# Layer 1's first six input-projection chunks from split rows and split weights

## The reference

```python
def hybrid_layer(h, p_i, ...):
    n = rmsnorm(h, g_mix)
    z = n @ w_in                     # 1024 -> 2432 columns, for the three mixers
    ...
    zc = z[..., o4:]                 # mixer C: GLU, causal conv of 31 taps, LayerNorm, silu
    glu = zc[..., :D_C] * jax.nn.sigmoid(zc[..., D_C:])
    conv_c, new_c = causal_dwconv(glu, prev_c, w_conv_c)
    y_c = jax.nn.silu(layernorm(conv_c + b_conv_c, g_ln_c, b_ln_c))
    y = jnp.concatenate([rmsnorm(y_a, ...), rmsnorm(y_b, ...), rmsnorm(y_c, ...)], axis=-1)
    h = h + y @ w_o
    h = h + ffn(rmsnorm(h, g_ffn))   # layer 0: dense SwiGLU; layer 1: top-2 of 8 experts
    h = h + jax.nn.sigmoid(rmsnorm(h, g_ple) @ w_ple_gate) * (p_i @ w_ple_proj)
    return h, new_a, new_c, v
```

## Time and profile before

| | us |
|---|---|
| median of three runs | 1104.04 (1102.91 to 1104.72) |
| the profiled execution | 1101.71 |
| its span, first to last instruction | 1100.1 |
| TensorE busy | 1077.6 (98%) |
| VectorE busy | 878.3 (80%) |
| ScalarE busy | 660.3 (60%) |
| mean granted TensorE clock | 0.996 |

### The profile page before, as it was taken

The page is one execution under the profiler, slowest core; times in us unless marked ns, Lnnn a source line. Parts: engine busy times, 40 slices in busy tenths (PEclk is TensorE's granted clock), DMA queues, the critical chain, the costliest instruction groups (busy, mean ns, idle before and its releaser), DMA issues.

```text
span 1100.1 us, 16067 instructions
## 1 busy us (share of the span) xinstructions
PE 1077.6 (98%) x5837; PEld 928.4 (84%) x5837; DVE 878.3 (80%) x1241; ACT 660.3 (60%) x830; POOL 43.5 (4%) x58
## 2 busy tenths in 40 slices
PE   9998999999999999999999999999999999999996
PEld 8887899999999887778888888888888888878785
DVE  5897566566667788349989999899998999999775
ACT  2204344344454113248888888887888878888674
POOL 1000000000000000000000010000100000002000
PEclk9999999999999999999999999999999999999998
DMA  8432644645542442339999999999999999999910
GB/s 336 152 145 79 229 154 163 263 154 174 193 170 77 169 153 86 146 116 349 367 363 405 357 391 373 357 399 366 385 374 350 414 363 379 376 368 408 382 71 40
DMA packets 24196, 291.48 MB, mean 265 GB/s; under 512 B 3160, under 2 KB 3192, under 8 KB 7376
## 3 DMA queue, kind: packets, MB, share of 16 engines
q1 hardware_dynamic: 21040, 280.32, 66.6%
q0 software_dynamic: 3104, 10.46, 2.7%
HBM read 283.98 MB, written 6.79 MB: 264 GB/s over the span
## 4 chain that ended last, share of the span: by engine, by line
PE 94%; DVE 2%; ACT 2%; DMA 1%; issue 1%; POOL 0%; DVEq 0%; ACTq 0%; POOLq 0%
PE bank L711 18%; PE bank L665 16%; PE bank L669 15%; PE bank L668 15%; PE bank L738 7%; PE bank L735 7%; PE bank L739 7%; PE bank L751 3%; DMA ring<-wstream 1%; PE bank L609 1%; PE bank L593 1%; PE bank L574 1%; DVE wlo L1269 0%; PE bank L761 0%; ACT whi L881 0%
## 5 line engine op out<-in xcount | busy, mean ns | idle before, releaser
L1269 DVE TENSOR_TENSOR wlo<-ring,whi 128x1024 fp32r<-128x1024 f32 x384 | 460.2, 1220 | 49.2 <-ACT whi L881 41.9
L881 ACT ACTIVATE whi<-ring 128x1024 fp32r<-128x1024 f32 x384 | 405.0, 1060 | 83.7 <-PE bank L665 72.0
L665 PE MATMUL bank<-whi,gh_hi 128*128 128x512 f32 x512 | 204.5, 399 | 0.1
L669 PE MATMUL bank<-whi,gh_lo 128*128 128x512 f32 x512 | 199.8, 390 | 0.0
L668 PE MATMUL bank<-wlo,gh_hi 128*128 128x512 f32 x512 | 199.5, 390 | 0.0
L735 PE MATMUL bank<-gh_hi,whi 128*128 128x264 f32 x480 | 138.0, 288 | 0.0
L738 PE MATMUL bank<-gh_lo,whi 128*128 128x264 f32 x480 | 136.0, 283 | 0.0
L739 PE MATMUL bank<-gh_hi,wlo 128*128 128x264 f32 x480 | 135.9, 283 | 0.0
L665 PEld LDWEIGHTS bank<-whi,gh_hi 128*128 128x128 f32 x512 | 96.2, 188 | 21.8 <-DVE wlo L1269 3.4
L669 PEld LDWEIGHTS bank<-whi,gh_lo 128*128 128x128 f32 x512 | 96.1, 188 | 20.9
L668 PEld LDWEIGHTS bank<-wlo,gh_hi 128*128 128x128 f32 x512 | 96.3, 188 | 18.4
(11 more groups left out here) (261 smaller groups left out, 1327.0 us busy)
## 6 DMA issues: line engine op xcount, KB each, us to landing
ring<-wstream SPq DMA_DIRECT2D x130, 2048.0 KB, 8.3
y_rows<-work POOLq DMA_DIRECT2D x7, 512.0 KB, 8.1
ring<-wstream SPq DMA_DIRECT2D x1, 1536.0 KB, 10.1
h<-x_in SPq DMA_DIRECT2D x2, 528.0 KB, 4.1
y_out<-work SPq DMA_DIRECT2D x2, 528.0 KB, 3.0
par<-par_in SPq DMA_DIRECT2D x2, 494.5 KB, 7.6
c_sample<-xc POOLq DMA_DIRECT2D x2, 372.0 KB, 3.8
stc<-state_in SPq DMA_DIRECT2D x2, 360.0 KB, 9.5
```

What stands on the lines that cost most here:

```text
L665: mm = pe.matmul(out[:, :], xh, whi[:, pos, cols_], start=(k == 0), stop=False)
L669: mm = pe.matmul(out[:, :], xl, whi[:, pos, cols_], start=False, stop=(k == last))
L881: nc.scalar.activation(whi[:, q % SPLITS, :], quarter_at(q), ACT.Copy).then_inc(S["hi"], 1)
L1269: v.tensor_tensor(wlo[:, q % SPLITS, :], quarter_at(q), whi[:, q % SPLITS, :].bitcast(F32), ALU.subtract).then_inc(S["lo"], 1)
```

## The change

Layer 1's six `zc` chunks are made by `project` in place of `project_fp32`. Its rows come from `hid_hi` and `hid_lo`, which VectorE writes in layer 0's gate, after `gz[k]`, for all eight k. `gz` is still made, since the thirteen `zab` chunks stay in float32; their first one now has the wait for it. The six quarters of `zc` weights join the list of those to be split. By `dense_quarters`, the first three of them are split in the gate's chunks 5, 6 and 7, the others in the `zc` stage, after the evacuations of chunks 0, 1 and 2.

```diff
-FP32_Q = [N_ZC + N_ZAB + KP * KD // QBLOCKS + KD] * DEPTH
-FP32_FROM = [NEED[_b["zc"]] - 1 for _b in BASE]
+FP32_Q = [(N_ZC if _l == 0 else 0) + N_ZAB + KP * KD // QBLOCKS + KD for _l in range(DEPTH)]
+FP32_FROM = [NEED[_b["zc" if _l == 0 else "zab"]] - 1 for _l, _b in enumerate(BASE)]
...
-                project_fp32(B["zc"], N_ZC, gz, S["gh_mix"])
-                project_fp32(B["zab"], 2 * CB, gz)
+                if l == 0:
+                    project_fp32(B["zc"], N_ZC, gz, S["gh_mix"])
+                else:
+                    project(B["zc"], N_ZC, *mix, S["gh_zc"])
+                project_fp32(B["zab"], 2 * CB, gz, S["gh_mix"])
...
                 for c in range(CC):
                     evacuate(B["zc"] + 2 * c, pp[:, 2 * c, :])
+                    low_upto(dense_quarters(B["zc"] + 2 * c))
                     some_taps(6 if c else 0, c)
                     evacuate(B["zc"] + 2 * c + 1, pp[:, 2 * c + 1, :])
+                    low_upto(dense_quarters(B["zc"] + 2 * c + 1))
                     some_taps(2 if c else 0, c)
...
                         mix_gain(l + 1, k)
+                        gain(l + 1, "g_mix", k, L[l + 1]["gh_zc"], hid_hi, hid_lo)
                         low_upto(dense_quarters(B["ple"] + k))
```

More of the change, by code:

```diff
@@ L299, in build @@
             "mean", "centred", "squared", "variance", "root_v", "scaled", "ln_b", "vt", "vtok", "mixed",
-            "y_c", "y_a", "y_b", "ys_sq", "y_ms", "y_root", "y_normed", "sq_ffn",
+            "y_c", "y_a", "y_b", "ys_sq", "y_ms", "y_root", "y_normed", "gh_zc", "sq_ffn",
             "gh_ple", "sq_ple", "sig_ple", "tails", "w_sT")} for l in range(DEPTH)]
```

## The result

The change takes 1107.97 us, the median of six runs (1107.06 to 1108.38), against 1103.06 us for the kernel before in six runs: a ratio of 1.0042, with a 95% interval from 1.003 to 1.0054. On a second occasion it was 1108.93 against 1102.75, ratio 1.0057 (1.0045 to 1.007). So it is slower, by 5 to 6 us. The profiled execution took 1107.93 us; its span, first to last instruction, is 1106.3.

What follows compares the result with a forecast made beforehand. TensorE bounds the kernel, with VectorE the slower engine in layer 0's gate. VectorE's delay 7.9, matmuls -3.8 and clock 2.3 give +6.4 us: 1110.4 us against the median, 1108.1 against the profiled execution; range 1106.3 to 1112.7.

Steps and rivals of the forecast that it cites:

- What bounds it: TensorE holds 94% of the chain; in layer 0's gate VectorE is slower, and its lateness there delays TensorE equally.
- The pairs, 7 x 0.80: Layer 0's gate: two row-part instructions per chunk on VectorE, seven times ahead of the last evacuation, 5.6 us later.
- the splits, 2 x 1.13: Gate chunks 5, 6 and 7: weight splits on VectorE, two ahead of the last evacuation, delay it 2.26 us.
- The matmuls, -3.8: Layer 1's six zc chunks: three float32r matmuls per block in place of float32 take 3.8 us off TensorE.
- the estimate of 5.3 us: Layer 1's six zc chunks: saving if three passes replaced four; worked out but not used in the forecast.
- Layer 1's splits: Three splits on VectorE in layer 1: its waits for TensorE absorb the lateness, so nothing is added.
- the ring: Weight transfers and slots: no transfer added, later slots asked for no later relative to TensorE, so nothing.
- The clock, +2.3: Layers' border: TensorE's waits drop its clock to 1.2 GHz as layer 1 starts, costing 2.3 us, bounds 0 and 4.6.
- The first wait ahead of it: Layers' border: TensorE waits some 3.6 us for squares of line 1134, before some 1 us for the last.
- the rival that the clock stays: Layers' border: the clock stays at 2.4 GHz, so only +4.05 us, 1108.1 us; chance 0.25.
- Hidden pairs: Layer 0's gate: row parts hide in VectorE's waits; fully, -3.8 us, 1100.2 us, chance 0.05; partly, within 0.2%, chance 0.05.
- VectorE late in layer 1: Layer 1: VectorE cannot use its 6.6 us of waits, line 1535 is 8.4 us late, 1112.4 us; chance 0.05.

Runs made afterwards that it cites:

- the filled run: The change plus 13 and 3 small matmuls into an unused bank where TensorE waits for squares: 1106.87 us, ratio 1.0043; run again, 1106.90 us, 1.0035.
- without pairs: The change without the two row-part instructions per gate chunk and the wait for them, so layer 1 computes other values: 1100.77 us, ratio 0.9978 to before.
- the pairs alone: The kernel before plus the two row-part instructions per gate chunk, results unused, no new splits, float32 matmuls: 1109.97 us, ratio 1.0069 to before.
- the splits behind the gate: The change with only its first three weight splits moved behind the gate's last chunk: 1108.43 us, ratio 1.0037 to before.
- the best version: The change with high row parts on ScalarE, low parts in VectorE's sigmoid wait, first three splits behind the gate: 1099.63 us, ratio 0.9965 to before.

## Why the prediction was right

**What bounds it.** VectorE was the slower engine in the gate, with no slack to layer 1. Right: 5.57 us of pairs in the gate alone made mixer B's rows later by 5.57 us.

**The pairs, 7 x 0.80, and the splits, 2 x 1.13.** Predicted 5.6 + 2.26, measured 5.57 + 2.27 apart and 7.87 together. The estimate of 4.06 us a chunk was met (4.05), because the same pair in the same shapes stood elsewhere in the trace.

**The matmuls, -3.8.** With the clock held up, first split matmul to first float32 one took 378.01 - 360.29 = 17.7 us in the filled run, 3.6 us less than six chunks at 3.56. That is 0.2 short of 3.8, and the delay ahead of them, 4.02 + 3.6 = 7.7, is 0.2 short of 7.9; that the sum came out at +4.02 for +4.05 owes something to the two cancelling. (The prediction's 353.0 for layer 1's first matmul was the start of a piece of the chain; the matmul itself starts at 352.85.) The Trainium skill (FP8 and Floating Point Precision, TensorE Precision Notes) counts four passes for true float32; the estimate of 5.3 us worked out from that would have been too high beside the 3.6 measured.

**Layer 1's splits and the ring, nothing.** Right: no bank or split holds TensorE among the chunks, and VectorE is back with TensorE before mixer B's rows, where it still waits 1.8 us.

**The clock, +2.3.** Right in kind, and in size 2.0 and 2.4 us up to mixer B's rows on two occasions. The first wait ahead of it was nearly as worked out (3.33 us for 3.6). The second was 0.22 for some 1 us, since the product before it, already at the lower clock, took 1.25 us for 0.45. The half-rate blocks took 0.66 us (three starts 0.22 apart) for 0.73. The size rests on luck in part: the one row of a rise was the program's beginning, where the profile's granted clock reads 1.00 and only the spacing of the matmuls tells of half pace:

```profile
2.00:3.00 1.00, 1.00 (x6) 1.00 (x6) 0.00 (x0) 0.22 (x1) 0.80 (x6) 1.00 0.74 152
```

In the change TensorE worked at the lower level from 360.25, the eighth product, to about 364.6, and half of these 4.35 us is 2.2. For the rival that the clock stays, I had taken's 434 to 441, with 1.7 us of waits in 7.4, as a sign for it; without pairs the clock fell behind 1.9 us of waits in 3, and with the pairs alone it stayed behind 1.5 in 3.

**The time.** +6.4 us was the sum; the profiled execution against the profiled one has 6.2, the medians 4.9 and on the second occasion 6.2. That the two traces agree so well with the sum is helped by the part behind the experts' first matmul, which took 607.3 and 607.4 us in them and 606.6 to 609.3 in all eleven. The 1108.1 us given against the profiled execution stands beside 1107.93 measured. The 1110.4 against the median is 2.4 too high on the first occasion and 1.5 on the second: the profiled execution of before lay 2.3 us under its median, that of the change did not. What makes executions of the kernel before differ by over 3 us (1101.33 to 1104.96 over all occasions) is open; the traces of the other kernels differ by such amounts in the experts' stage.

**The rivals.** The clock that stays would have given 1108.1, and the measured median alone is nearer to that than to the forecast; the trace, with its granted clock of 0.50, and the filled run show that the clock did fall. Hidden pairs: refuted by the pairs alone. VectorE late in layer 1: refuted by its wait at mixer B's rows.

## What to carry to other kernels

Before moving work from TensorE to another engine, find in that stage's timeline which engine starts its next round without a wait: work put on that one costs its full length in each round, and here seven times 0.8 us on VectorE outweighed the 3.6 us won on TensorE. The same work cost the gate nothing with its first half on ScalarE and its second in a wait of 0.49 us that VectorE had in each round. Splits moved behind the last chunk of the loop left the gate 2.3 us shorter, though the first of them can hold up the next stage, by 0.75 us in one run. A wait on TensorE that such work makes can cost more than its own length: here layer 1 began at half rate, which cost 2.0 and 2.4 us up to mixer B's rows.

## What I had not expected of the hardware

The granted clock fell at the border in kernels where TensorE waited only some 2 us, in two pieces. Without pairs, it fell behind waits of 1.21 and 0.76 us, with 1.07 us busy of 3.00; with the pairs alone, it stayed at 1.00 behind waits of 1.04 and 0.76, with 1.52 busy of 3.00. At the experts' beginning all eleven traces have the same work in the 3 us ahead of it, 2.15 or 2.16 us busy with a last wait of 0.84 or 0.85; the clock fell there in four of them (both filled runs, the splits behind the gate, and the best version) and stayed at 1.00 in seven. So like stretches of work came out either way, and a single profile can't tell which way is usual.
